# Input weights in half transfers, identity products where TensorE stands, norm rows loaded later, and the result of the expert loop signalled in front of its branch

## The reference, cut to what matters

```python
for layer in range(2):
    mix = _even_mixer(x, w_in, pool_w, pool_scale, w_out) if layer == 0 else _rwkv7_mixer(x, mu, w_r, w_k, w_v, ...)
    x = _layer_norm(ALPHA * x + mix, ln_mix_g[layer], ln_mix_b[layer])
    ff = routed + shared        # 8 of 64 SwiGLU experts of width 256 per token, and one shared expert
    x = _layer_norm(ALPHA * x + ff, ln_ffn_g[layer], ln_ffn_b[layer])

def _even_mixer(x, w_in, ...):  hcat = x @ w_in      # 1024 x 2048: pool u, q, k, v
def _rwkv7_mixer(x, ...):       r = xr @ w_r; k = xk @ w_k; v = xv @ w_v; low-rank w, a, g; ...
```

## Time and profile before

| | |
|---|---|
| runs, median (lowest to highest) | 1355.78 us (1354.37 to 1360.9) |
| the profiled execution | 1359.91 us, of which the span of its records is 1358.2 us |
| TensorE matmul busy | 1316.4 us, 97% of the span, 9712 records |
| VectorE, ScalarE, GpSimd busy | 443.5, 264.6, 83.0 us |
| DMA | 450.35 MB, mean 332 GB/s; 422 GB/s in the expert stages |
| chain that ended last | TensorE 94%, VectorE 4%, the rest 1% each |
| granted TensorE clock, mean | 0.995 |

### The profile page before, as it was taken

The page is one execution under the profiler, slowest core; times in us unless marked ns, Lnnn a source line. Parts: engine busy times, 40 slices in busy tenths (PEclk is TensorE's granted clock), DMA queues, the critical chain, the costliest instruction groups (busy, mean ns, idle before and its releaser), DMA issues.

```text
span 1358.2 us, 23440 instructions
## 1 busy us (share of the span) xinstructions
PE 1316.4 (97%) x9712; PEld 750.6 (55%) x9712; DVE 443.5 (33%) x1002; ACT 264.6 (19%) x524; POOL 83.0 (6%) x124
## 2 busy tenths in 40 slices
PE   8999999999999999998999999999999999999997
PEld 6889544434434343437777998834344343444433
DVE  2245222222212222217571666522222122222213
ACT  1231211111111111112432230211111111111111
POOL 7203000000000000001001301100000000000001
PEclk9999999999999999998999999999999999999999
DMA  4698799999999999991734006798999999999993
GB/s 155 181 331 325 283 377 396 423 421 422 422 422 421 422 422 422 421 377 33 237 109 173 4 4 248 289 385 349 423 422 422 422 422 422 422 422 422 422 421 148
DMA packets 98661, 450.35 MB, mean 332 GB/s; under 512 B 16033, under 2 KB 45345, under 8 KB 48929
## 3 DMA queue, kind: packets, MB, share of 16 engines
q1 hardware_dynamic: 98592, 449.34, 82.5%
HBM read 448.26 MB, written 1.05 MB: 331 GB/s over the span
## 4 chain that ended last, share of the span: by engine, by line
PE 94%; DVE 4%; issue 1%; DMA 1%; ACT 1%; POOL 0%; SPq 0%; DVEq 0%; PEldq 0%; ACTq 0%
PE PS L1882 31%; PE PS L1921 17%; PE PS L1929 10%; PE PS L1853 7%; PE PS L550 4%; PE PS L513 3%; PE PS L1380 2%; PE PS L1417 2%; PE PS L1394 2%; PE PS L1901 1%; PE PS L2002 1%; PE PS L1567 1%; PE PS L1893 1%; PE PS L535 1%; PE PS L1551 1%
## 5 line engine op out<-in xcount | busy, mean ns | idle before, releaser
L2234 DVE TENSOR_TENSOR y_parts<-PS,y_parts 128x512 fp32r<-128x512 f32 x128 | 88.5, 691 | 216.6 <-ACT y_parts L2136 216.6
L2208 DVE SCALAR_TENSOR_TENSOR AR<-AR,PS 128x256 f32<-128x256 f32 x64 | 30.7, 480 | 386.4 <-ACT AR L2114 386.4
L1929 PE MATMUL PS<-y_parts,token_map 128*128 128x512 f32 x496 | 146.5, 417 | 0.0
L1882 PE MATMUL PS<-AR,xT 128*64 128x512 f32 x512 | 115.7, 593 | 5.6 <-issue 5.5
L1929 PEld LDWEIGHTS PS<-y_parts,token_map 128*128 128x128 f32 x496 | 83.5, 188 | 60.9 <-issue 50.3
L1921 PE MATMUL PS<-AR 128*64 128x512 f32 x512 | 116.9, 599 | 0.0
L1921 PE MATMUL PS<-RING,AR 128*64 128x512 f32 x496 | 116.9, 599 | 0.0
L1882 PE MATMUL PS<-AR 128*64 128x512 f32 x512 | 115.5, 592 | 0.0
L2136 ACT CAST y_parts<-PS 128x512 fp32r<-128x512 f32 x128 | 74.9, 586 | 172.0 <-PE PS L1921 172.0
L1882 PE MATMUL PS<-RING,xT 128*64 128x512 f32 x480 | 108.1, 592 | 0.0
L1882 PE MATMUL PS<-RING,AR 128*64 128x512 f32 x480 | 108.1, 592 | 0.0
(11 more groups left out here) (322 smaller groups left out, 1485.3 us busy)
## 6 DMA issues: line engine op xcount, KB each, us to landing
RING<-in_moe_w_gate SPq DMA_DIRECT2D x64, 1024.0 KB, 11.8
RING<-in_moe_w_up SPq DMA_DIRECT2D x64, 1024.0 KB, 13.8
AR<-in_moe_w_gate SPq DMA_DIRECT2D x64, 1024.0 KB, 13.1
AR<-in_moe_w_up SPq DMA_DIRECT2D x64, 1024.0 KB, 15.2
AR<-in_moe_w_down SPq DMA_DIRECT2D x64, 1024.0 KB, 13.9
RING<-in_moe_w_down SPq DMA_DIRECT2D x62, 1024.0 KB, 15.0
AR<-in_ab_w_in SPq DMA_DIRECT2D x8, 1024.0 KB, 5.8
AR<-in_rw_w_o SPq DMA_DIRECT2D x4, 1024.0 KB, 6.0
```

The source lines that it names most:

```text
L1882: ins = nc.tensor.matmul(PS[s * B:(s + 1) * B, 4, :], gathered(k)[:, c:c + B], gate_and_up(slots[s])[:, k, :, :], start=(k == 0), stop=(k ...
L1929: ins = nc.tensor.matmul(PS[:, 2 * t + h, :], OHT[:, half, t, :], YS[:, n, h * 512:(h + 1) * 512], start=False, stop=True, skip_group_chec ...
L2208: nc.vector.scalar_tensor_tensor(out=HH[0:2 * B, :].rearrange("p (k j) -> p k j", k=FT), in0=by_row(SIL[0:2 * B, :]), scalar=GC[:, buf:buf ...
L2234: nc.vector.tensor_tensor(YS[:, 1, h * 512:(h + 1) * 512], PS[:, 5 + h, :], YS[:, 0, h * 512:(h + 1) * 512], ALU.subtract).then_inc(q["low ...
```

## The change

The input weights go as two transfers of 512 KB each, with a semaphore for each half, and TensorE waits for the second half in front of the fifth product of a tile. Six products of the identity with itself stand ahead of the first turning of x, two behind it, and ten behind the turning of tile 0 in layer 1; nothing reads what they write. At the end of the experts, `s_res` is raised by the last scatter products themselves, the shared expert's products come next, and the branch behind them. In `sp_mix1` the first wait is for `s_scl` (the scale of tile 0 in the norm behind the experts) instead of the whole sum, and the norm rows are issued behind `w_rec`. GpSimd's wait for the whole sum becomes one for the normed x; two semaphores that doubled others (`count_ready`, `keys_scaled`) are gone, and a helper that nothing called.

```diff
         def load_chunk(sp, src, b, c):
-            sp.dma_start(chunk(b), src[:, :, ds(c * CB, CB)]).then_inc(s_wl[b], 16)
+            for half, loaded in enumerate((s_wl[b], s_wr[b])):
+                ks = slice(4 * half, 4 * half + 4)
+                sp.dma_start(chunk(b)[:, ks, :], src[:, ks, ds(c * CB, CB)]).then_inc(loaded, 16)
...
-                            if k == KT // 2 and b == 0 and c == 0 and x_whole:
-                                x_whole()
+                            if k == KT // 2 and c == 0:
+                                pe.wait_ge(s_wr[b], 16 * i + 16 * (base // 2 + 1))
...
+        def busy(bank, count):
+
+            for n in range(count):
+                nc.tensor.matmul(PS[:, bank, (n % 4) * P:(n % 4) * P + P], ident[:, :], ident[:, :], start=True, stop=True)
+
         def pe_mix0(pe):
+            pe.wait_ge(s_const, 1)
+            busy(0, 6)
             pe_transpose(pe, 0, 0)
             pe_transpose(pe, 0, 1)
+            busy(0, 2)
             pe.wait_ge(s_xT, 4)
             project_channels(pe, xT, 0, 6, 0)
...
         def sp_mix1(sp):
-            sp.wait_ge(s_res, 4 * TT)
+            sp.wait_ge(s_scl, 1)
...
-            load_ln(sp, 2)
             for dst, src in [(g1, a["rw_g1"][0].rearrange("(p k) c -> p k c", k=KT)), (g2a, a["rw_g2"][0][0:P, :])]:
                 sp.dma_start(dst, src).then_inc(s_lg, 16)
...
             for c in range(4):
                 sp.wait_ge(s_pj, TK + 2 * c + 2)
                 load_rw(sp, w_rec, c)
+            load_ln(sp, 2)
...
             g.wait_ge(moe_shared["x_split"], TT)
-            g.wait_ge(s_res, 4 * TT)
+            g.wait_ge(s_za, TT)
...
             pe_transpose(pe, 2, 0)
+            busy(6, 10)
...
                         for t in range(TT):
                             ins = nc.tensor.matmul(PS[:, 2 * t + h, :], OHT[:, 1, t, :], YS[:, n, h * 512:(h + 1) * 512],
                                                    start=False, stop=True, skip_group_check=True)
+                            if n == 1 and t == 0:
+                                ins.then_inc(s_res, 1)
                 ins.then_inc(q["scattered"], 1)
+                for h in range(2):
+                    shared_down(pe, 1, h).then_inc(s_res, 1)
                 with pe.If(most > CAP):
                     pe_over(pe)
-                pe.wait_ge(q["scattered"], PAIRS + past["scattered"])
-                pe.sem_inc(s_res, 2)
-                for h in range(2):
-                    shared_down(pe, 1, h).then_inc(s_res, 1)
...
-                v.sem_inc(q["count_ready"], 1)
```

More of the change, by code:

```diff
@@ L317, in program @@
         s_wl = [sem(f"mixer_chunk_loaded{b}") for b in range(2)]
+        s_wr = [sem(f"mixer_chunk_rest_loaded{b}") for b in range(2)]
         s_wo = [sem(f"mixer0_out{c}_loaded") for c in range(2, 4)]
@@ L482, in swapped, with project_channels @@
             return x.rearrange("p (t a r) -> p t a r", t=TT, a=2)[:, :, ::-1, :]
-        def project_heads(pe, x, base, chunks, tile0, x_whole=None):
+        def project_channels(pe, x, base, chunks, tile0):
             with pe.Fori(0, chunks // 2) as i:
@@ L520, in project_tokens @@
                 for b in range(2):
-                    pe.wait_ge(s_wl[b], 16 * i + 16 * (base // 2 + 1))
+                    for loaded in (s_wl[b], s_wr[b]):
+                        pe.wait_ge(loaded, 16 * i + 16 * (base // 2 + 1))
                     for t in range(TT):
@@ L756, in loaded @@
                     pe.wait_ge(s_wl[c - 2], 16 * 5)
+                    pe.wait_ge(s_wr[c - 2], 16 * 5)
             pe.wait_ge(s_cat, 4)
@@ L977, in dve_mix1 @@
                 ins = V.tensor_scalar(T1[:, k, :], KTT[:, k, :], VEC[:, V_KK, k:k + 1], None, ALU.mult)
-            ins.then_inc(r["keys_scaled"], 1)
+            link(ins)
             v.wait_ge(s_lh, 1)
@@ L993, in dve_mix1 @@
             V.reciprocal(SSQ, SSQ).then_inc(r["norm_ready"], 1)
-            v.wait_ge(r["keys_scaled"], 1)
+            link.sync()
             V.tensor_tensor(flat2(KTT), flat2(KTT), flat2(T2), ALU.mult).then_inc(r["keys_mixed"], 1)
@@ L1734, in pe_core @@
             project_out(pe, KTT, WO, 1, loaded, last_chunk=lambda: pe_transpose(pe, 3, 0))
-        once = ["logits_done", "scores_ready", "mask_ready", "rank_done", "rank_ready", "count_ready",
+        once = ["logits_done", "scores_ready", "mask_ready", "rank_done", "rank_ready",
                 "first_gates", "shared_gate", "shared_gate_up", "shared_silu", "shared_hidden", "gates_split", "pads_cleared"]
@@ L1832, in loads @@
                         load_rw(sp, w_key, c)
-                sp.wait_ge(q["count_ready"], 1 + past["count_ready"])
+                sp.wait_ge(q["rank_ready"], 1 + past["rank_ready"])
                 most = nc.sync.value_load(cnti[0:1, 2 * l:2 * l + 1], min_val=0, max_val=T)
@@ L2406, in dve_over @@
                     v.sem_inc(q["over_dve"], 1)
+                v.wait_ge(q["over_free"], rounds + 1)
+                nc.vector.memset(F1[0:E, 1, 0:1], 0.0)
                 link.leave(NOV // 2)
```

7 lines of the change are left out of this document (3 added, 4 removed).

## The result

The changed kernel took 1344.82 us, the median of four runs (1343.25 to 1345.98), against 1358.34 for the kernel before on the same chip (four runs, 1354.37 to 1361.11; 1355.78 was the median of three of them). The ratio is 0.990, with a 95% interval of 0.988 to 0.992: faster, by 13.5 us in the medians. 1342 had been predicted. The profiled execution after is the fastest of the four, 1343.25 us, with a span of 1341.4.

What follows compares the result with a forecast made beforehand. TensorE bounds the kernel, its matmuls busy 1316.4 of 1358.2 us; 4.8 + 4.8 + 1.7 + 3.8 + 0.7 = 15.8 us off 1359.9 or the median 1355.78 gives 1344.1 or 1340.0, middle 1342; 8-in-10 range 1337 to 1349.5.

Steps and rivals of the forecast that it cites:

- Start: Input projection: halved transfers and eight products start it 1.8 us earlier and remove 3.0 of slow pace; bounds 0.5 to 5.5.
- Rival B: Start: clock does not rise early, projection starts early but slow, only 1.5 us of 4.8 come; 1345.3 us, 13%.
- Loop end: Layer 0 experts' end: signals ahead of the branch gain 4.8 us; ten products behind tile 0's turning avoid 1.7 of half clock.
- rival A: Layer 0 experts' end: the branch stalls again, gain there 2.1 us instead of 4.8; 1345 us, 20%.
- SP's order: Layer 1 mixer: earlier receptance weights remove a 2.11 us wait and 1.7 of half clock behind it; 3.8, bounds 2.1 to 3.8.
- End: End of layer 1: VectorE's statistics and the shared products move up, 0.7 us gained; bounds 0.3 and 0.8.
- C: Expert stages: transfers give the gain back as a wait at their end, only 0.7 us stays; 1355 us, 8%.
- D: Expert loop: its code no longer stays held, each pass fetches for 3.6 us, 43 in all; slower, 1385 us, 4%.

Runs made afterwards that it cites:

- e5: Changed kernel without the six and two identity products around the first turning of x; 1349.64 us, ratio 0.9930.
- e3: Kernel before plus 65 waits on an already long-given signal at the start of TensorE's list, no products added; 1357.74 us, ratio 1.0007.
- e11: Changed kernel with 65 empty waits in place of the eight identity products at the start; 1350.35 us, ratio 0.9948.
- e2: Kernel before plus only the scatter's signals and shared products ahead of the branch, with the changed first waits of SP and GpSimd; 1353.56 us, ratio 0.9961.
- e9: Changed kernel with its 18 identity products written as transposes; 1348.62 us, ratio 0.9946.
- r1: Kernel before, unedited, run again for a second profile; single run of 1358.71 us.
- e1: Kernel before plus only the six and two identity products (and one wait) around the first turning of x; 1358.54 us, ratio 1.0005.
- r2: e1 once more, unedited, for a second profile; single run of 1358.54 us.
- e8: Changed kernel with the norm rows loaded ahead of the gate weights again; 1348.51 us, ratio 0.9932.
- e4: Changed kernel with the loop end of before: branch first, then signals and shared products; 1346.63 us, ratio 0.9916.

## Why the prediction was right, and where not

*Start, 4.8 predicted.* 5.6 between the two profiles, just above the upper bound of 5.5; 4.6 against the second profile of before. The slow pace was sized right (3.0, and 2.9 went). The earlier start was 2.7 instead of 1.8, because the turning itself ran at full clock, which I had kept for the bound. No row gave the 0.8 us by which I put the first half's landing at about 8; it ended the projection's wait at 7.77. The reason was half right: e5 and e3 show the clock full without any product, and e3 without halves. What held it down in both profiles of before is not shown: the wait of 2.4 to 2.5 us for the chunk goes with it, but e11 was slow behind a wait of 0.99. Rival B, by which the projection stays slow, failed here (42.26 us to the first scores). It needed turning not to count. x is turned by transposes (L341, one record each), and in e2, e3 and e5 they were all that TensorE had done before it ran the projection at 2.4 GHz; in e9 transposes alone did it too. The Trainium skill says that a transpose does not count as busy time for the clock in the way a product does (TensorE: Matmul & The Clock Gate, Part 4: PE-mode transpose). For float32 transposes four traces here speak against that: by it, e2, e3, e5 and e9 would have begun the projection slowly, as before, r1 and e11 did. That products ahead of them bring the full clock sooner stands: the turning took 2.4 to 2.8 us in the profiles with products (the seven of them), 3.5 to 3.7 in those without. In e9 it took 3.68, but its six transposes were half the work and 1.49 us of waiting followed them, so it doesn't compare the two kinds.

*Loop end, 4.8 plus 1.7.* Last scatter to keys gave 5.07 us, keys to low ranks 1.38. The size is right against the profile that I had. Against the second profile of before it is 2.1, since the branch was 2.31 us there and no half clock lay on the shared products. I priced one run's branch as if it were the kernel's. The step that failed is where I put the new branch: "from about 612.3", 4.7 us behind the first of the last scatter products (607.58), so that a long one would lie "in front of the turning of tile 0" and cost the gain down to 2.1 (rival A). In after, e2, e5 and e9 TensorE's sequencer came to it 1.5 us behind that product, with the shared products still queued. So the branch lies beside them and not behind them, and e2, e5 and e9, with 1.8 to 2.7 us, lost nothing between scatter and turning (5.68 us as with 0.35). A branch of 3.6 us in layer 0 did not come up under the new order and was not tried.

So rival A failed twice over: the branch was short, and a long one up to 2.7 us costs nothing. That it would be short I drew from the place in the list, "now some 50 instructions longer ahead of it". At that place it was short in all five profiles. But e1, r2 and e3 show that the place does not fix it, and e1 in layer 1 that a longer list can also bring the long branch; part of that step was luck.

*SP's order, 3.8.* 3.87: 2.18 before the receptance and 1.69 behind. The first part is in every profile with the old order (2.0 to 2.7 us), and e8 gives it for the order alone (2.8). The half clock behind it came in four of these seven (before, e1, e3, r2) and not in r1, e2 and e8, the longest wait of all. So the 1.7 are chance, as the remark in the prediction had it, and an average run gains about 1 of them, an estimate from these counts.

*End, 0.7.* 0.78, as worked out; e2 alone gives 0.77, e4 takes it back.

*Rivals C and D.* C fails: scores to last scatter is 552.0 before and after (551.8 to 552.5 over all 14 profiles), and every microsecond won ahead of it arrived. D fails: one packet of the instruction queue came in 291 us of the expert loop.

*The size.* The sum was 15.8 us; the two profiles' spans differ by 16.75, the medians by 13.5. The rest is the choice of runs: the profiled execution before lay 1.6 us above its median, the one after 1.6 below. I had thought the profiled run 4 us high and its half-clock stretches more than most, and took 1342 between two bases. That was wrong: a fourth run put the median of before at 1358.34, r1 took 1358.71 with as much half clock between the start and the last norm (10.2 us in both), and 46 further runs of the kernel before lie from 1353.0 to 1362.6. From 1358.34 the sum gives 1342.5, 2.3 less than measured; what it has too much is in the terms above that stood on one profile's branch and clock. That the middle of two bases, one of them too low, came out 2.8 us off is in part luck.

The stretch from the values to the turning, whose code was not changed but for its place, took 148.2 to 153.3 us over the 14 profiles. e3 had the most, with three half-clock stretches in it (at 738.8, 796.8 and 813.9 us, 1.7 us each). Of the eight profiles of the changed kernel and its variants two (e5, e8) had any there, of the six of before and its variants four. The clock isn't all of it: e4 took 150.0 us with none, 1.7 more than after. Where the 1.6 us of the changed kernel's other runs lie is not shown, as it was profiled once; their mean granted clock (0.997 to 0.998, against 0.998) leaves room for one stretch of half clock at most, an estimate: 3.4 us of it lower the mean by 0.0013.

No version of these beat the changed kernel; every part that was taken out of it made the time longer or left it within the measurement.

## What to carry to other kernels

Put the signals, and some microseconds of queued products, ahead of a branch rather than behind it: the branch's code may have to be fetched, how much of the fetch is left varies from run to run, and queued work covers it. Padding the code to move the stall is no cure: with the list 32 instructions longer the stall stood in the other layer in two profiles (e1, r2), and in the third (e3) it stayed half in the first. Before a stall or a clock stretch in one profile is priced, a second profile of the same kernel helps to tell which of them are the kernel's and which that run's.

## What the runs showed of the hardware

- The instruction queue moves packets of 16 KB, 55 in the kernel before and 56 in the changed one. The branch ended 2.3 to 2.6 us after a packet's start in the ten cases where it took over 0.5 us, and took 0.34 to 0.47 in the other 18. In the three longest the packet starts 1.0 us behind the branch's start (3.3 to 3.6 us in all), as if the jump itself had asked for it.
- The clock can be full after float32 transposes alone: the projection ran at full pace from its first record in e3 (3.49 us of them) and e5 (3.59), and at half in before, r1 and e11 (3.65 to 3.68). It fell behind a wait of 3.92 us that followed work at full clock (r2).
- Behind 3.4 to 3.7 us of idle time before the keys, or on the way there, the clock fell each time; with the ten products and 1.1 to 1.2 us it fell in two of six profiles (e9's wait was 2.3 us, without a fall). The remaining chance is not explained.
